# A router that turns the residual itself and takes the rows' factors on its logits, and expert blocks in three interleaved runs that keep their weights in place

## What is computed

```python
x = x + gate1 * (mixed @ w_out)
h2 = rms_norm_2(x, norm2_g) * (1.0 + scale2) + shift2
# router: group softmax (4 groups), top 1; expert softmax in the group (8), top 2
expert = g_idx * 8 + e_idx                    # 2 of 32 experts for each token
# the 4096 (token, expert) pairs are sorted by expert; each expert's part is
# padded to whole blocks of 128 rows
def expert_block(rows, e):
    xb = t_pad[rows]
    hid = silu(xb @ w_gate[e]) * (xb @ w_up[e])
    return hid @ w_down[e]
x = x + gate2 * (sum of the weighted rows of the blocks)
```

## Time and profile before

| | |
|---|---|
| median of 3 runs | 3672.84 us (3671.2 to 3678.9) |
| the profiled execution's own time | 3669.79 us |
| its span | 3667.9 us |
| busy share of the span | PE 94%, DVE 47%, ACT 29%, POOL 27% |
| granted TensorE clock, mean | 0.981 |
| projection and router, from the first matmul of tile 0 | 2749 us to 3058 us |
| experts | 3058 us to the end |

### The profile page before, as it was taken

How to read it: one execution, slowest core, us unless ns; L and a number is a source line. 1 busy time by engine, 2 the same in 40 slices (tenths; PEclk the granted TensorE clock), 3 DMA queues, 4 the chain that set the end, 5 groups by cost and what they waited for, 6 DMA issues and landing times. The chain is left out here.

```text
span 3667.9 us, 32753 instructions
## 1 busy us (share of the span) xinstructions
PE 3460.3 (94%) x11181; PEld 1792.6 (49%) x11181; DVE 1707.4 (47%) x4073; ACT 1046.7 (29%) x2551; POOL 1000.7 (27%) x1395
## 2 busy tenths in 40 slices
PE   4999899999999999999999998899999986999998
PEld 3754355555444644444444444555664433444443
DVE  4656633343355484326655556644454553222222
ACT  3122122221110362002234446643332221222221
POOL 0277767500000393000000002655651001222221
PEclk8999999999999999999999999999999998999999
DMA  3133444433245112222221000000102215999997
GB/s 140 57 131 138 145 157 155 140 126 109 97 160 176 64 36 81 107 88 92 81 85 35 23 9 12 1 1 1 69 25 104 98 75 214 325 336 337 330 331 237
DMA packets 115562, 451.55 MB, mean 123 GB/s; under 512 B 15635, under 2 KB 43155, under 8 KB 103356
## 3 DMA queue, kind: packets, MB, share of 16 engines
q1 hardware_dynamic: 91484, 370.18, 28.3%
q0 software_dynamic: 18432, 58.74, 6.0%
q10 hardware_dynamic: 5472, 20.45, 1.5%
HBM read 340.28 MB, written 117.42 MB: 125 GB/s over the span
## 5 line engine op out<-in xcount | busy, mean ns | idle before, releaser
L142 PE MATMUL pst<-arena 128*128 128x512 f32 (+4 forms) x6554 | 2694.8, 568 | 48.5 <-DMA arena<-in_w_exp 25.5
L142 PEld LDWEIGHTS pst<-arena 128*128 128x128 f32 x6554 | 1243.9, 196 | 1337.6 <-issue 1232.4
L164 POOL TENSOR_TENSOR arena<-arena 128x4 f32<-128x4 f32 (+7 forms) x784 | 403.3, 514 | 455.7 <-DVE arena L2060 395.3
L164 DVE TENSOR_TENSOR arena<-arena 128x1 f32<-128x1 f32 (+8 forms) x1260 | 460.1, 366 | 95.0 <-ACT arena L2290 20.1
L147 PE MATMUL pst<-arena 128*128 128x128 f32 x2161 | 328.1, 286 | 100.3 <-DVE arena L246 52.5
L147 PEld LDWEIGHTS pst<-arena 128*128 128x128 f32 x2161 | 260.7, 146 | 278.5 <-issue 153.2
L1286 POOL TENSOR_SCALAR arena<-arena 128x384 f32<-128x384 f32 (+1 forms) x128 | 151.7, 1213 | 555.8 <-DVE arena L1278 554.6
L153 ACT ACTIVATE arena<-pst,arena 128x128 f32<-128x128 f32 (+1 forms) x630 | 244.8, 485 | 92.7 <-PE pst L147 90.2
L2237 POOL TENSOR_SCALAR arena<-arena 128x512 f32<-128x512 f32 (+3 forms) x160 | 218.6, 1390 | 150.5 <-DVE arena L164 137.2
L167 DVE TENSOR_SCALAR arena<-arena 128x1 f32<-128x1 f32 (+11 forms) x581 | 141.2, 243 | 194.9 <-DMA arena<-in_bc 80.0
L152 ACT ACTIVATE arena<-pst 128x512 f32<-128x512 f32 (+4 forms) x250 | 124.7, 518 | 323.9 <-PE pst L142 197.1
(11 more groups left out here) (200 smaller groups left out, 2070.4 us busy)
## 6 DMA issues: line engine op xcount, KB each, us to landing
arena<-in_w_exp SPq DMA_DIRECT2D x48, 3072.0 KB, 11.8
arena<-in_w_ada SPq DMA_DIRECT2D x48, 512.0 KB, 4.8
rotd<-arena POOLq DMA_DIRECT2D x32, 512.0 KB, 4.0
arena<-rotd SPq DMA_DIRECT2D x32, 512.0 KB, 4.7
arena<-sgd SPq DMA_DIRECT2D x16, 1024.0 KB, 7.1
arena<-pwd SPq DMA_DIRECT2D x32, 416.0 KB, 5.6
pwd<-arena SPq DMA_DIRECT2D x16, 576.0 KB, 6.1
h2d<-arena SPq DMA_DIRECT2D x17, 512.0 KB, 2.9
```

The costliest lines, as they stand in the source:

```text
L142: x = t.do.matmul(o, l, r, start=(i == 0), stop=(i == len(pairs) - 1))
L164: own(v, s).tensor_tensor(o, a, b, op).then_inc(*inc(s, *event))
```

## The change

Router: PE turns `x3` instead of `xn`, in the middle of the next tile; ACT's copy keeps the scale and loses the shift; the logits are multiplied by `rin` afterwards on DVE, and the shift's part of the logits is made once (`te_o2_shift`, 8 matmuls) and added to the bias. Turning `LT` back and adding the halves become one set of four matmuls with a matrix `fold` (two identities on top of each other). The pick of batch b moves from tile 4b+6 to 4b+5, and what follows it moves by one tile too. The store of `xn` for the experts stays.

Experts: slot s = 3a + b now runs block a + 16b (table `sB`), so that each of the three weight buffers sees a run of 16 neighbouring blocks. From slot 3 on the weights are loaded by POOL with two indirect DMAs (`w_up`, 16 KB rows; `w_down`, 8 KB rows), whose row numbers `wI` are moved past the table's end where the block three slots before has the same expert: such rows aren't loaded. The up part waits only for up of the block three before. Gathers go three slots ahead instead of two. SP loads slots 0 to 2 only.

```diff
             t.wait_ge(*at("o2_ac", "LT", b))
-            trs(t, [(bank(6)[:, u * 128:(u + 1) * 128], LT[:, u * 128:(u + 1) * 128]) for u in range(4)]
-                ).then_inc(*inc("o2_pe", "lg", b))
+            t.wait_ge(*at("rt_po", "made"))
+            for u in range(4):
+                o = t.do.matmul(bank(6)[:, u * 128:u * 128 + 36], LT[:, u * 128:(u + 1) * 128], fold, start=True, stop=True)
+            o.then_inc(*inc("o2_pe", "lg", b))
+        def te_o2_shift(t):
+            t.wait_ge(*at("ld_par", "b_rt"))
+            mm(t, bank(6)[:, 0:36], [(bc(modc[:, 16 + k], 1, [128, 128]), wr[:, k, :]) for k in range(8)]
+               ).then_inc(*inc("o2_pe", "shift"))
...
+        def ve_o2_shift(v):
+            q = "o2_ve"
+            v.wait_ge(*at("ld_par", "b_rt"))
+            v.wait_ge(*at("o2_pe", "shift"))
+            tt(v, q, brb, brb, bank(6)[:, 0:36], ADD, "shift")
         def ve_o2_logits(v, b):
-            q = "o2_ve"
-            b6, o = bank(6).rearrange("p (a n) -> p a n", a=4), lg[:, 4 * b:4 * b + 4, :]
+            q, f = "o2_ve", slice(4 * b, 4 * b + 4)
             v.wait_ge(*at("o2_pe", "lg", b))
-            v.wait_ge(*at("ld_par", "b_rt"))
-            tt(v, q, o, b6[:, :, 0:36], bc(brb, 1, [128, 4, 36]), ADD)
-            tt(v, q, o, o, b6[:, :, 64:100], ADD, "lg", b)
+            tt(v, q, lg[:, f, :], bank(6).rearrange("p (a n) -> p a n", a=4)[:, :, 0:36], bc(rin[:, f], 2, [128, 4, 36]), MUL)
+            tt(v, q, lg[:, f, :], lg[:, f, :], bc(brb, 1, [128, 4, 36]), ADD, "lg", b)
+        def te_o2_turn(t, j):
+            t.wait_ge(*at("o2_ve", "x3", j, 1))
+            for hb in range(2):
+                t.wait_ge(*at("o2_ac", "xT", j - 1, hb))
+                trs(t, [(bank(4 + hb)[:, u * 128:(u + 1) * 128],
+                         x3t(j)[:, (4 * hb + u) * 128:(4 * hb + u + 1) * 128]) for u in range(4)]
+                    ).then_inc(*inc("o2_pe", "xT", j, hb))
...
-            for i in range(NT + 3):
+            for i in range(NT + 2):
+                if i in (5, 9, 13, 17):
+                    te_o2_logits(t, i // 4 - 1)
                 if i < NT:
                     tk_ = slice(i * 128, (i + 1) * 128)
                     for c in range(2):
...
                         mm(t, bank(2 * c), [(qn[:, k, tk_], WO2[c][:, k, :]) for k in range(4)])
                     if i == 0:
                         te_o2_sums(t, 0)
+                if i in (5, 9, 13, 17):
+                    te_o2_logits_turn(t, i // 4 - 1)
+                if 1 <= i <= NT:
+                    te_o2_turn(t, i - 1)
+                if i < NT:
                     t.wait_ge(*at("ld_mL", "mL", 3))
                     for c in range(2):
                         mm(t, bank(2 * c + 1), [(mL[k][:, tk_], WO2[c][:, 4 + k, :]) for k in range(4)]
                            ).then_inc(*inc("o2_pe", "x3", i, c))
                     if i % 4 == 2 and i < 12:
                         te_o2_sums(t, i // 4 + 1)
-                if i in (5, 9, 13, 17):
-                    te_o2_logits(t, i // 4 - 1)
-                if i in (6, 10, 14, 18):
-                    te_o2_logits_turn(t, i // 4 - 1)
-                if 1 <= i <= NT:
-                    j = i - 1
-                    t.wait_ge(*at("o2_ve", "xn", j))
-                    for hb in range(2):
-                        t.wait_ge(*at("o2_ac", "xnT", j - 1, hb))
-                        trs(t, [(bank(4 + hb)[:, u * 128:(u + 1) * 128],
-                                 xn[j % 2][:, (4 * hb + u) * 128:(4 * hb + u + 1) * 128]) for u in range(4)]
-                            ).then_inc(*inc("o2_pe", "xnT", j, hb))
-                if i in (8, 12, 16):
-                    te_rt_ranks(t, i // 4 - 2)
+                if i == 1:
+                    te_o2_shift(t)
+                if i in (7, 11, 15):
+                    te_rt_ranks(t, i // 4 - 1)
...
-                if i in (6, 10, 14, 18):
+                if i == 1:
+                    ve_o2_shift(v)
+                if i in (5, 9, 13, 17):
                     ve_o2_logits(v, i // 4 - 1)
                     ve_rt_pick(v, i // 4 - 1)
+                if i in (7, 11, 15):
+                    ve_rt_weights(v, i // 4 - 1)
                 if i in (8, 12, 16):
-                    ve_rt_weights(v, i // 4 - 2)
-                if i in (9, 13, 17):
                     ve_rt_rows(v, i // 4 - 2)
...
-                if i in (7, 11, 15):
+                if i in (6, 10, 14):
                     ac_rt(a, i // 4 - 1)
-                if i == 17:
-                    ac_o2_logits(a, 3)
-                if i < NT:
-                    a.wait_ge(*at("o2_ve", "x3", i, 1))
-                    sq_sum(a, q, junk5, x3t(i), ss[:, i:i + 1], "ss", i)
-                if i in (5, 9, 13):
+                if i in (5, 9, 13, 17):
                     ac_o2_logits(a, i // 4 - 1)
                 if 1 <= i <= NT:
                     j = i - 1
                     a.wait_ge(*at("o2_pe", "logits", j // 4 - 1))
                     for hb in range(2):
-                        a.wait_ge(*at("o2_pe", "xnT", j, hb))
+                        a.wait_ge(*at("o2_pe", "xT", j, hb))
                         for u in range(4):
                             k = 4 * hb + u
                             acopy(a, xnT4[hb][:, u, j % 4 * 128:j % 4 * 128 + 128], bank(4 + hb)[:, u * 128:(u + 1) * 128],
-                                  scale=modc[:, 24 + k:25 + k], bias=modc[:, 16 + k:17 + k]
-                                  ).then_inc(*inc(q, *(["xnT", j, hb] if u == 3 else [])))
+                                  scale=modc[:, 24 + k:25 + k]).then_inc(*inc(q, *(["xT", j, hb] if u == 3 else [])))
+                if i < NT:
+                    a.wait_ge(*at("o2_ve", "x3", i, 1))
+                    sq_sum(a, q, junk5, x3t(i), ss[:, i:i + 1], "ss", i)
...
+            p.do.iota(sB[:, 0:48].rearrange("p (a b) -> p a b", a=16), [[1, 16], [16, 3]], base=0, channel_multiplier=0,
+                      allow_small_or_imprecise_dtypes=True).then_inc(*inc("rt_po"))
+            p.do.iota(sB[:, 48:64], [[1, 16]], base=48, channel_multiplier=0, allow_small_or_imprecise_dtypes=True
+                      ).then_inc(*inc("rt_po"))
+            p.wait_ge(*at("const_po", "ident"))
+            p.do.tensor_tensor(fold, ident[:, 0:36], ident[:, 64:100], ADD).then_inc(*inc("rt_po"))
...
-            trs(t, [(bank(6)[0:1, 0:128], bcol[:, 1:2])]).then_inc(*inc("rt_pe", "bE"))
-            t.wait_ge(*at("o2_ac", "xnT", NT - 1, 1))
...
-            ts(v, q, bcol[:, 1:2], bcol[:, 1:2], 31.0, None, MIN, BYP, "owner")
+            ts(v, q, bcol[:, 1:2], bcol[:, 1:2], 31.0, None, MIN, BYP)
+            ts(v, q, dg, sB, bcol[:, 2:3], bcol[:, 1:2], ALU.is_equal, MUL, "owner")
             own(v, q).tensor_copy(nbI, pen[:, 31:32]).then_inc(*inc(q, "nb"))
             v.wait_ge(*at("rt_pe", "bE"))
             v.do.tensor_copy(bE[0:1, :], bank(6)[0:1, 0:64]).then_inc(*inc(q, "bE"))
+            ts(v, q, wf, bank(6)[:, 0:64], 128.0, bcol[:, 2:3], MUL, ADD)
+            tt(v, q, same[:, 3:64], wf[:, 3:64], wf[:, 0:61], ALU.is_equal)
+            stt(v, q, same[:, 3:64], same[:, 3:64], bcol[:, 3:4], wf[:, 3:64], MUL, ADD)
+            own(v, q).tensor_copy(wI[:, 3:64], same[:, 3:64]).then_inc(*inc(q, "wI"))
...
-                tt(v, q, big[:, kk, :], bc(blk[:, k, :], 2, [128, 16, 64]), bc(io128[:, 0:64], 1, [128, 16, 64]),
+                tt(v, q, big[:, kk, :], bc(blk[:, k, :], 2, [128, 16, 64]), bc(sB, 1, [128, 16, 64]),
                    ALU.is_equal)
...
-        def sp_moe_load(s, b):
+        def sp_moe_first(s):
             for i in range(2):
                 s.wait_ge(*at(f"st_out{i}", "x3", NT - 2 + i))
             s.wait_ge(*at("rt_ve", "bE"))
-            s.wait_ge(*at("moe_pe", "down", b - 3, 1))
-            e = s.do.value_load(bE[0:1, b:b + 1], min_val=0, max_val=31)
-            s.do.dma_start(WX[b % 3], T["w_exp"][bass.ds(e, 1), :, :].rearrange("a p n -> p (a n)")
-                           ).then_inc(*dma(f"moe_wx{b % 3}", "wx", b))
+            for b in range(3):
+                e = s.do.value_load(bE[0:1, b:b + 1], min_val=0, max_val=31)
+                s.do.dma_start(WX[b][:, 0:4096], T["w_up"][bass.ds(e, 1), :, :].rearrange("a p n -> p (a n)")
+                               ).then_inc(*dma(f"moe_wf{b}", "up", b))
+                s.do.dma_start(WX[b][:, 4096:6144], T["w_down"][bass.ds(e, 1), :, :].rearrange("a p n -> p (a n)")
+                               ).then_inc(*dma(f"moe_wf{b}", "down", b))
+        def po_moe_load(p, b, part):
+            p.wait_ge(*at("rt_ve", "wI"))
+            for i in range(3):
+                p.wait_ge(*at(f"moe_wf{i}", "down", i))
+            if part == "up":
+                p.wait_ge(*at("moe_pe", "up", b - 3))
+                o, w = WX[b % 3][:, 0:4096], T["w_up"]
+            else:
+                p.wait_ge(*at("moe_pe", "down", b - 3, 1))
+                o, w = WX[b % 3][:, 4096:6144], T["w_down"]
```

(42 more changed lines are left out.)

13 lines of the change are left out of this document (9 added, 4 removed).

## The result

| | before | changed |
|---|---|---|
| median (4 runs each) | 3673.64 us (3671.2 to 3678.9) | 3629.14 us (3625.8 to 3632.89) |
| ratio, 95% interval | | 0.9877 [0.9865, 0.9889] |
| the profiled execution's own time, its span | 3669.79, 3667.9 us | 3625.8, 3624.0 us |

Faster by 44.5 us. A second comparison on the chip gave 0.9882 [0.9865, 0.9899]. The forecast was 3636 us with a range of 3625 to 3662; the time lies 7 us under the forecast and inside the range. The size is right, but the reason given for the largest part of it is not, as the experiments show.

A forecast was written before the change was run, and what follows sets the result against it. The experts' stage was taken as bound by DMA as much as by PE. From 3669.8 us, 33 (experts) and 2 (router) come off: 3634.8, stated as 3636 us because the runs' median lies 3 us higher; range 3625 to 3662.

The forecast's parts named there:

- Experts, the size: Experts' stage: every period falls from 12.12 us to PE's own 11.41 us, 33 us saved.
- Experts, the reason: Experts' stage: DMA's 569 us of work bound it as much as PE; 33 loads for 48 leave 448 us.
- 27 us of new lead: Experts' stage: up's load is issued 27 us before its use, where 11.8 + 4.5 us are needed.
- Experts, added on POOL: Experts' stage: two more indirect DMAs a block keep POOL busy 4.7 of 11.4 us.
- Router, in the loop: Router's tile loop: stalls after picks shrink by 3.0 us, added PE instructions cost more; sum +1.7 us.
- Router, behind the loop: After the router's last tile: earlier turn and copy give -4.9 us, five added instructions before `idT` cost +1.1 us.
- POOL's cover before tile 0: Before tile 0: five more small POOL instructions take 0.7 us, and the 1.1 us of cover hold, barely.
- Dearer queue: Rival, experts' stage: POOL's loads cost q0's 4.19 us per MB, periods total 597 us, 3696 us; chance 0.08.
- the point of 3.5: Experts' stage: PE stays the bound while POOL's loads cost up to 3.5 us per MB.
- The skip saves nothing: Rival, experts' stage: left-out rows are moved all the same, only the router's 2 us remain, 3668 us; chance 0.04.
- POOL's order holds the loads up: Rival, experts' stage: scatter waits between POOL's loads lose 21 of the 33 us, 3656 us; chance 0.11.
- The fixed 2.0 us for each DMA from POOL: Experts' stage: unoverlapped, it would add 120 us for 60 loads, bring DMA to 568 us and leave no gain.

The follow-up runs named there:

- no_skip: The changed kernel with all 48 blocks' weights loaded, same order and queue: 3634.05 us, ratio 0.9899 to the kernel before; first to last tanh 534.9 us.
- after_again: The changed kernel measured once more beside the kernel before on the same chip: 3630.11 us, ratio 0.9882.
- late_no_skip: The changed kernel without skip and early release, POOL loading all 45 later slots in two pieces: 3639.56 us, ratio 0.9928 to the kernel before.
- split_only: The kernel before with each load cut in two DMAs (up, then down), still on SP at the old release: 3637.70 us, ratio 0.9917.
- experts_only: The kernel before with only the experts' part of the change, its router left as it was: 3626.89 us, ratio 0.9886.

## Why the prediction was right, and where it was not

- **Experts, the size.** -33 was forecast, -34.5 measured. The step that carried it held: all periods become PE's 11.4 us (11.38 measured), and the change can't give more. The 1.5 us above the forecast are PE's own period, 11.38 us and not the 11.41 of the sum, over 47 periods.
- **Experts, the reason.** The step that failed is the pricing of DMA: 62.6% and 28.0% of the time turned into 2.62 and 4.19 us per MB, a sum of 569 us, and from it "bound by DMA as much as by PE". By these prices no_skip, with 48 loads at q1's price or dearer, has the 569 us of DMA work of before or more, and no gain in the stage; it took 534.9. That the sum met the 569 us of periods said only that some packet was nearly always under way. The bytes saved (94.8 MB loaded by POOL, as counted) freed DMA to 0.84 and bought no time once the loads were cut.
- **What should have been read.** The prediction had both numbers of the right mechanism: the landing of 11.8 us and the block's pieces. It set the landing against 27 us of new lead and took that as cover, yet never against the old window, 11.6 us less SP's 0.7 to issue, where the miss was. That a cut of the load alone is nearly enough (32.0 of 34.5 us) could then have been foreseen.
- **Experts, added on POOL.** 4.7 us busy a block was forecast; 192.07 us over 41.6 blocks are 4.6. Nothing waits for it.
- **Router, in the loop.** Forecast +1.7, with stalls of 0.6, 0.6 and 1.4; they are 1.04, 0.56 and 1.35. The shift's 16 instructions cost less: they stand in one row of 48, which takes 15.69 us where 32 alone take 13.90, so 1.8 us for a forecast of 2.4. From tile 0 to the last residual it is 258.3 us for 259.0, 0.7 less where 1.0 more was forecast (1.7, less the 0.75 that the residual comes earlier).
- **Router, behind the loop.** Residual to DVE's start on the logits: 14.7 to 9.8 us, -4.8; the forecast was -4.9 with 0.75 for the fold on top, -4.2. From there to `idT` 23.6 to 25.3 us, +1.7; forecast +1.1. The five added instructions were counted, but not that PE's matmul for `dg` takes 0.69 us with a wait of 1.81, where the single transpose took 0.37 with 1.45. In all -4.1 for a forecast of -2, within its bounds, and in part luck: the logits ran at the full clock, which they did in only two of the nine profiles of this router; in after_again it is -1.2.
- **POOL's cover before tile 0.** It held, "barely": 0.26 us.
- **Outside the terms.** 4.9 us of the span lie ahead of tile 0, in code that nobody touched. The profiles of the other kernels show this stretch to wander by more than that, so I take it as chance. It isn't fully settled: the stages' sum, 39.1 us, gives a ratio of 0.9894, the two comparisons gave 0.9877 and 0.9882, and only the second's interval holds 0.9894.
- **The rivals.** *Dearer queue*: q0 took 75.2% of 595 us for 136.72 MB; less the 176 us of gathers and scatters that leaves 2.9 us per MB for the loads, below the point of 3.5. But this measure tells nothing, as above. Up's part did land 2.3 us later in late_no_skip than on SP, which is covered here. *The skip saves nothing*: the rows are left out; and had they not been, the time would have been no_skip's, not 3668 us. *POOL's order holds the loads up*: four waits for a scatter, 13.3 us, none of which reached PE. The fixed 2.0 us for each DMA from POOL that the Trainium skill states ("DMA: Bandwidth & Descriptors", section "Anatomy of one DMA — SWDGE (gpsimd) path") would have added an estimated 180 us for the 90 of no_skip. This case's traces don't bear that out: PE never waits for a DMA in no_skip's stage, so whatever is fixed about a DMA did not add up there.

## What to carry to other kernels

When an engine waits again and again, by a microsecond or so, for a transfer, compare the transfer's time with the window from its release to its first use, before counting bytes: here 0.7 us to issue and 11.8 to land stood against a window of 11.6, and two DMAs with the part wanted first in front gave 32 of 34.5 us. A DMA share near 1 did not tell here that no more would go through; doubt it until a run with more bytes is slower. And look for the part of a change that does the work: a plainer version, loads cut and released early, gather one block further ahead, all on the queues that were there, equals the stage of the elaborate one.

## What the runs showed of the hardware

- The busy share of the 16 DMA engines read 0.98, 1.01 and 1.01 at 331, 353 and 369 GB/s.
- Loads issued by POOL as indirect DMAs of 16 and 8 KB rows ran at 353 GB/s (no_skip) and 346 (late_no_skip) together with gathers and scatters, SP's loads at 349 to 354. POOL is busy 0.99 us for each.
- In POOL's queue up's part landed after 10.8 us (late_no_skip), on SP after 8.5 (split_only), at 346 and 352 GB/s. The queue is not their only difference.
- A load was issued 0.7 us after the down that frees its buffer on SP (before) and 0.8 on POOL (late_no_skip).
- Whole rows left out by the bounds check moved nothing: 94.8 MB for 30 of 45 loads.
- Behind stalls of 3.04 and 3.03 us PE's same 32 instructions took 14.00 us at a granted clock of 1.00 (before) and 15.70 at 0.66 in their first 4 us (experts_only). Behind waits of 2.15 us the same 16 instructions of the logits took 3.63, 5.33 or 6.23 to 6.52 us.
- POOL's eight one-hot rows took 4.66 us with DVE mostly idle and 8.08 beside a busy DVE.
